# Four modulation chunks moved from layer 0's mixer to the end of its experts, the rest respread, and a scratch tile moved

## What is computed

```python
def adaln_layer(x, cond, g_mix, g_ffn, ada_w, ada_b, mixer, moe_params):
    mod = (silu(cond) @ ada_w + ada_b)[:, None, :]      # (1024) @ (1024 x 6144)
    sh1, sc1, g1, sh2, sc2, g2 = split(mod, 6)
    out, state = mixer(rms_norm(x, g_mix) * (1 + sc1) + sh1)
    x = x + g1 * out
    x = x + g2 * hier_moe(rms_norm(x, g_ffn) * (1 + sc2) + sh2, *moe_params)
```

## Time and profile before

| | before |
|---|---|
| median of 3 runs (lowest, highest) | 1665.0 us (1661.41, 1667.53) |
| the profiled execution, its own time | 1667.2 us |
| its span, first to last instruction | 1665.4 us |
| mean granted TensorE clock, as a share of 2.4 GHz | 0.947 |
| PE busy, DVE busy, ACT busy, POOL busy | 91%, 27%, 18%, 9% |
| HBM traffic | 319 GB/s over the span |
| layer 0: projection and mLSTM / attention and output / experts | to about 250 / 250 to 377 / 377 to 857 us |
| between the layers | 857 to 878 us |

### The profile page before, as it was taken

How to read it: one execution, slowest core, us unless ns; L and a number is a source line. 1 busy time by engine, 2 the same in 40 slices (tenths; PEclk the granted TensorE clock), 3 DMA queues, 4 the chain that set the end, 5 groups by cost and what they waited for, 6 DMA issues and landing times.

```text
span 1665.4 us, 21436 instructions
## 1 busy us (share of the span) xinstructions
PE 1516.3 (91%) x8387; PEld 723.5 (43%) x8387; DVE 445.5 (27%) x1055; ACT 304.9 (18%) x649; POOL 145.8 (9%) x200
## 2 busy tenths in 40 slices
PE   5999887979999999999958998896999999999991
PEld 4455784444433333333314555544333333333330
DVE  0012586433111111111123025633311111111113
ACT  3100225211111111111121005511111111111112
POOL 1002111100000000000005000100000000000001
PEclk9999887978999999999988999997999999999995
DMA  9999962245999999999969522103999999999982
GB/s 349 331 335 179 384 223 104 81 177 220 428 427 428 428 428 428 428 427 427 428 252 309 184 101 77 53 28 144 408 428 428 427 428 427 429 428 428 427 345 117
DMA packets 82919, 521.56 MB, mean 313 GB/s; under 512 B 10130, under 2 KB 11610, under 8 KB 56240
## 3 DMA queue, kind: packets, MB, share of 16 engines
q1 hardware_dynamic: 69536, 485.58, 71.4%
q0 software_dynamic: 13328, 35.22, 6.9%
HBM read 511.01 MB, written 20.22 MB: 319 GB/s over the span
## 4 chain that ended last, share of the span: by engine, by line
PE 88%; DVE 7%; ACT 2%; DMA 1%; issue 1%; POOL 0%; POOLq 0%; DVEq 0%; ACTq 0%
PE psum L896 26%; PE psum L909 14%; PE psum L877 10%; PE psum L543 6%; PE psum L842 5%; PE psum L565 5%; PE psum L562 3%; PE psum L902 3%; PE psum L467 2%; PE psum L889 2%; PE psum L883 2%; PE psum L764 1%; PE psum L509 1%; PE psum L751 1%; PE psum L789 1%
## 5 line engine op out<-in xcount | busy, mean ns | idle before, releaser
L896 PE MATMUL psum<-ring,area_t 128*64 128x512 f32 x1024 | 449.9, 592 | 1.8 <-issue 0.9
L897 PE MATMUL psum<-ring,area_t 128*64 128x512 f32 x1024 | 450.0, 593 | 0.0
L896 PEld LDWEIGHTS psum<-ring,area_t 128*64 128x64 f32 x1024 | 140.1, 137 | 291.8 <-issue 291.8
L909 PE MATMUL psum<-ring,area_t 128*64 128x512 f32 x1024 | 235.6, 602 | 2.3 <-DVE area_t L1864 2.3
L1835 DVE COPY area_q<-psum 64x512 f32<-64x512 f32 x64 | 44.4, 694 | 567.2 <-PE psum L897 567.2
L877 PE MATMUL psum<-area_h,area_t 128*64 128x512 f32 x768 | 180.8, 607 | 3.0 <-DVE area_t L1849 3.0
L2048 POOL DMA_INDIRECT pair_rows<-area_q,idx x64 | 62.4, 975 | 932.3 <-ACT area_q L1267 932.3
L897 PEld LDWEIGHTS psum<-ring,area_t 128*64 128x64 f32 x1024 | 140.2, 137 | 0.0
L909 PEld LDWEIGHTS psum<-ring,area_t 128*64 128x64 f32 x1024 | 69.1, 137 | 123.2 <-issue 123.2
L1257 ACT ACTIVATE area_q<-psum 64x512 f32<-64x512 f32 x64 | 37.8, 590 | 403.3 <-PE psum L897 403.3
L877 PEld LDWEIGHTS psum<-area_h,area_t 128*64 128x64 f32 x768 | 56.6, 140 | 113.7 <-issue 110.5
(11 more groups left out here) (265 smaller groups left out, 1396.7 us busy)
## 6 DMA issues: line engine op xcount, KB each, us to landing
ring<-in_moe_w SPq DMA_DIRECT2D x192, 2048.0 KB, 14.8
ring<-in_ada_w SPq DMA_DIRECT2D x24, 2048.0 KB, 20.0
ring<-in_na_w_in SPq DMA_DIRECT2D x6, 2048.0 KB, 17.2
ring<-in_ab_w_in SPq DMA_DIRECT2D x5, 2048.0 KB, 18.7
area_m<-mod_ready POOLq DMA_DIRECT2D x6, 1024.0 KB, 9.3
area_q<-pair_rows POOLq DMA_DIRECT2D x6, 1024.0 KB, 7.3
ring<-in_ab_w_out SPq DMA_DIRECT2D x2, 2048.0 KB, 20.8
area_g<-mod_ready POOLq DMA_DIRECT2D x4, 1024.0 KB, 8.8
```

The lines of the kernel that those rows point to most:

```text
L896: pe.matmul(banks[2 + u][0:64, :], lhsT, w1[:, k, :], start=(k == 0), stop=(k == KT - 1))
L897: mm = pe.matmul(banks[2 + u][64:128, :], lhsT, w3[:, k, :], start=(k == 0), stop=(k == KT - 1))
L909: mm = pe.matmul(banks[6 + u][64 * j:64 * j + 64, :], hidT[u][:, k, :], w2[:, k, 512 * j:512 * j + 512], start=(k == 0), stop=(k == 3))
```

## The change

The table of steps changes, four points of PE's program get a new `ada_step` or lose one, and ACT's copies, DVE's `modulation(5)` and POOL's round trip for group 5 move with it:

```diff
-        ADA_STEPS = ((("in", 0), 2), ... (("in", 4), 2), (("in", 5), 2), ("turned", 2), ("summed", 1), ("scored", 1), (("stage", 0), 1), (("stage", 1), 1), (("stage", 2), 2))
+        ADA_STEPS = ((("in", 0), 2), ... (("in", 4), 0), (("in", 5), 2), ("turned", 2), ("summed", 1), ("scored", 1), ("updated", 1), ("last", 1), ("gap", 4))
-        mixed = area_m[:, 4608:5632].rearrange("p (b n) -> p b n", b=2)
+        mixed = area_q[:, 4608:5632].rearrange("p (b n) -> p b n", b=2)
# stream: layer 1's list begins with the four chunks
             if l:
+                stream += [("ada",) + q for q in ADA_AT["gap"]]
                 stream += [("in", 1, c) for c in NA_ORDER]
# PE, project_na
+                pe.wait_ge(M["y_copied"], EXPERTS)
+                ada_step("gap")
# PE, mlstm: stage 2 behind direction 0; stage 0 ahead of the sums; the three stage steps go
                         if s == 2 and d == 0:
                             sums(s, 0)
+                            ada_step("last")
...
                             update_products(s, d)
+                        if s == 0:
+                            ada_step("updated")
                         sums(s, 0)
                         sums(s, 1)
-                        ada_step(("stage", s))
...
-                ada_step(("stage", 2))
# ACT, mlstm and finish_layer
+                    if s == 0:
+                        ada_copies("updated")
...
                         duplicate_keys()
+                        ada_copies("last")
...
+                    if l == 0 and t == 0:
+                        ada_copies("gap")
                     act.wait_ge(S["x_moe"], NT * l + t + 1)
# DVE: out of attention, to the start of layer 1
-                    if l == 0 and i in (5, 10):
-                        modulation(4 if i == 5 else 5)
+                    if l == 0 and i == 5:
+                        modulation(4)
...
                 if l:
+                    modulation(5)
                     copy_na()
# POOL: group 5's round trip, from the mLSTM's end to the start of layer 1
-            for G in range(4, 6):
-                store_ada(*divmod(G, 3))
-                finish_mod(G)
+            store_ada(1, 1)
+            finish_mod(4)
...
+                    store_ada(1, 2)
+                    finish_mod(5)
                     pool.wait_ge(S["h_ready"], NT * 3)
+                    pool.wait_ge(S["cmod_stored"], 160)
```

More of the change, by code:

```diff
@@ L271, in build @@
         over_landed = [sem(f"over{l}_landed") for l in range(2)]
-        ADA_STEPS = ((("in", 0), 2), (("in", 1), 2), (("in", 2), 2), (("in", 3), 2), (("in", 4), 2), (("in", 5), 2), ("turned", 2), ("summed", 1), ("scored", 1), (("stage", 0), 1), (("stage", 1), 1), (("stage", 2), 2))
+        ADA_STEPS = ((("in", 0), 2), (("in", 1), 2), (("in", 2), 2), (("in", 3), 2), (("in", 4), 0), (("in", 5), 2), ("turned", 2), ("summed", 1), ("scored", 1), ("updated", 1), ("last", 1), ("gap", 4))
         ADA_AT, ADA_GROUPS = {}, {}
@@ L291, in build @@
                 stream.append(("in", 0, _step[1]))
-            stream += [("ada",) + q for q in ADA_AT[_step]]
+            if _step != "gap":
+                stream += [("ada",) + q for q in ADA_AT[_step]]
         for l in range(2):
             if l:
+                stream += [("ada",) + q for q in ADA_AT["gap"]]
                 stream += [("in", 1, c) for c in NA_ORDER]
@@ L440, in _ @@
             load_overflow(0)
-            for n in range(NUM["in", 1, NA_ORDER[0]], NUM["moe", 1, 0]):
+            for n in range(NUM[("ada",) + ADA_AT["gap"][0]], NUM["moe", 1, 0]):
                 if n == NUM["in", 1, NA_ORDER[1]]:
@@ L573, in turn_na @@
                 if n == 0:
+                    pe.wait_ge(S["ada_copied"], 5)
                     pe.wait_ge(S["na_ctx_loaded"], 16)
@@ L716, in turn_queries @@
                     pe.wait_ge(S["ctx_v"], 16)
-                    pe.wait_ge(S["ada_copied"], 5)
+                    pe.wait_ge(S["ada_copied"], 4)
                 for t in range(NT):
@@ L1170, in mlstm @@
                         b_squares(2)
-                    ada_copies(("stage", s))
+                    if s == 0:
+                        ada_copies("updated")
                     if s == 1:
@@ L2072, in _ @@
                 if l == 0:
-                    pool.wait_ge(S["cmod_stored"], 160)
+                    pool.wait_ge(S["cmod_stored"], 128)
                 load_G(l, 0)
```

## The result

The changed kernel takes 1668.96 us (median of 6 runs, 1668.52 to 1672.93), the kernel before on the same chip 1666.0: ratio 1.0028, 95% interval 1.0015 to 1.0042. So the change costs about 3 us where a gain of 0.3 us was forecast. That is a small slowdown inside the forecast range, but neither interval holds 1.0000, the ratio of no change. All ratios here compare fast runs with fast runs; one run of e3, 3183.21 us, was slow and is not in its ratio.

What follows compares the result with a forecast made beforehand. The chain was taken as 88% PE, so moving chunks off it should pay: -6.2 us in layer 0 and +5.9 between the layers give -0.3 us, forecast 1664.7 us, range 1657.0 to 1672.0.

Steps and rivals of the forecast that it cites:

- Projection, -3.7: Projection's end: PE loses two ada chunks and all of their 3.7 us counts.
- mLSTM stages, -1.7: mLSTM stages 0 and 1: two single chunks move into PE's gaps, shortening DVE's waits by 1.7 us together.
- mLSTM's end, -0.6: Between mLSTM and attention: two chunks go, but attention waits for the state stores, so only 0.6 us is gained.
- rival B: mLSTM's end: state stores do not hold attention back, so about 7 us counts instead of 0.6; 1658.3 us, chance 0.17.
- PE idle for some 5 us: Sign expected ahead of ACT's first copy of attention, with that copy at 251 to 252 us.
- Start of attention: Layer 0: ACT's first copy of attention was to come at 251 to 252 us instead of 257.12.
- Attention, -0.2: Attention: DVE loses three tiny operations of modulation(5), about 0.2 us less.
- Layer 0 together, -6.2: Layer 0 up to its experts: projection, mLSTM, mLSTM's end and attention sum to 6.2 us less.
- Between the layers, PE nothing: Between the layers: four chunks, at most 14.6 us, fit PE's idle 21.24 us and cost PE nothing.
- Transfers, +5.9: Between the layers: queued weight chunks slow the last scatter by 3.2 us and each pair megabyte by 1.9; 5.9 us more.
- Rival D: Between the layers: the queue costs more than layer 0's 6.2 us, up to 13.4, 1672.2 us; chance 0.17.
- Rival C: Between the layers: pair traffic is let through, the queue costs only 0 to 3 us, about 1660 us; chance 0.13.

Runs made afterwards that it cites:

- e3: Kernel before plus four unused 2 MB loads between the layers, ahead of layer 1's projection chunks; 1675.7 us, ratio 1.0045 to the kernel before.
- e5: Kernel before with the mLSTM's n and m stores issued later, during layer 1's attention; 1664.6 us, ratio 0.9986 to the kernel before.
- e10: Kernel before plus two unused 2 MB loads between the layers; 1668.4 us, ratio 1.0008 to the kernel before.
- e12: Kernel before run again unchanged, for a second profile; 1665.6 us, ratio 0.9998.
- e1: Changed kernel run again unchanged, for a second profile; 1668.6 us, ratio 1.0019 to the kernel before.
- e2: Changed kernel with its four chunk loads between the layers cut to an eighth, products and waits kept; 1664.5 us, ratio 0.9984 to the kernel before.
- e4: Changed kernel with the mLSTM's n and m stores issued later, during layer 1's attention; 1664.2 us, ratio 0.9986 to the kernel before.
- e6: Changed kernel with the four chunks at the mLSTM's end instead of between the layers; 1668.3 us, ratio 1.0012 to the kernel before.
- e9: Changed kernel with the four chunks in layer 0's output projection and routing, n and m stored later; 1653.7 us, ratio 0.9929 to the kernel before.
- e11: Kernel before plus four unused 2 MB loads issued only when the last scatter has landed; 1671.5 us, ratio 1.0024 to the kernel before.
- e8: Changed kernel with the four chunks in layer 0's output projection and routing instead of between the layers; 1659.1 us, ratio 0.9947 to the kernel before.
- e7: Changed kernel with the four chunks at the mLSTM's end and n and m stored later; 1661.8 us, ratio 0.9975 to the kernel before.

## Why the prediction was wrong

*Projection, -3.7.* Right. From the first projection product to the mLSTM's first piece all six profiles with the old steps take 112.5 us, the eight others 108.7: -3.8.

*mLSTM stages, -1.7.* Wrong. From the mLSTM's first piece to POOL's issue of the C store, just ahead of n's, it is 66.9 to 68.1 us in the six profiles with the old mLSTM (first, e3, e5, e10 to e12; mean 67.4) and 67.1 to 69.7 in the eight with the new one (first, e1, e2, e4, e6 to e9; mean 68.3): 0.9 longer, though the two ranges overlap. The chunk ran in the gap at the high clock, as hoped (1.95 us at 205.77), but then PE had nothing until DVE was done. Windows 40 us behind the mLSTM's first piece, at about the same work, in the first profiles before and changed:

```profile
213.60:218.60 5.00, 3.39 (x31) 3.20 (x30) 4.61 (x8) 0.00 (x0) 0.00 (x0) 1.00 1.06 396
```

```profile
214.40:219.40 5.00, 4.21 (x20) 3.91 (x20) 4.21 (x10) 0.00 (x0) 0.00 (x0) 0.50 0.78 334
```

The granted clock there is 0.50 instead of 1.00, and the products on which DVE waits take up to twice as long (2.07 us at 213.31, 1.21 before). My bound of 0, "a chunk at the low clock in a gap gives the wait back", named another piece: the chunk was not slow, the work behind it was. But that this costs the time is not shown. e11 has the old mLSTM, 0.50 in this window too and one of the shortest stretches (67.0 us to the C store); e4 has the new mLSTM, 0.98 there and 67.1. Why the 1.7 us did not come stays open.

*mLSTM's end, -0.6.* The mechanism is right, and with it rival B falls: attention waits for the stores, whose landing is there to the tenth of a microsecond (e4). The size is lost in the scatter: the n store is issued 13.3 us before attention's first copy in the changed kernel (first, e1, e2: 11.9 to 14.3) and 13.4 with the two chunks (first, e3, e10 to e12: 12.4 to 14.5). Rival B's 8.5 us were never PE time alone (e5). Two readings were wrong. "The engines are busy with something" is not what the profile shows: from 247.5 to 254.5 us it has a single packet in the kernel before, one of the instruction queue. And the sign "PE idle for some 5 us" does not follow from my own terms: products that end at 246.80 - 5.4 = 241.4 and a copy at 251 to 252 leave 9 to 10 us. 9.4 to 11.7 were found.

*Start of attention.* Forecast 6.0 us earlier, found 2.3: 192.0 us behind the first projection product (three profiles, 189.7 to 193.6) instead of 194.3 (five, 192.9 to 196.1). In these same profiles the mLSTM takes 1.6 us longer up to the n store, and -3.8 + 1.6 - 0.1 is this -2.3.

*Attention, -0.2.* Here 3.4 us came that I had not seen: 123.6 us from its first copy to the first expert product instead of 127.0. DVE's work on attention is 0.7 us shorter; the rest is spread over attention and the output projection and is not settled. The cut at attention's first copy is a soft one: e1, which starts attention 3 to 4 us earlier than the other two profiles of the changed kernel, takes 125.5 us from there, they 122.2 and 123.0. e6, whose chunks stand ahead of attention again, takes 127.1.

*Layer 0 together, -6.2.* 315.6 us (315.2 to 315.8) instead of 321.3 (318.0 to 324.1) from the first projection product to the first expert product, so -5.7. The sum held by luck, since two misses cancelled: the mLSTM gave nothing, and attention gave 3.4 us that I had not seen.

*Between the layers, PE nothing.* Right: PE idles 16 us behind its last chunk.

*Transfers, +5.9.* This is the step that failed. The sum of a to d grew from 21.3 to 29.0: **+7.7**. The scatter's landing was taken from a neighbour, 3.2; it cost 4.4. The pairs were priced by bandwidth, 4.8 us a megabyte from the start of the kernel, 1.9 more for each. The first paid 3.3 and the second only 0.3. So my sum followed the second megabyte (7.0 less 1.1 of slack), where in fact the first decides: 4.4 + 3.3 = 7.7. What costs is the beginning of each transfer behind which something waits, not its share of the engines once it runs. The Trainium skill's rule on packets (DMA: Bandwidth & Descriptors, Queues, rings and completion order) fits the share that the pairs then had. They got 86.2% of the engines' time beside the weights' 17.2%, and the second megabyte came in 3.2 us. But the 4.3 us that the prediction drew from it for the whole stretch were still further off, since they price the share as well. The same page of the Trainium skill (Latency and other measured facts) names a longer memory access at high load, up to 2 us. The trace agrees in direction at most and shows 3 to 4.5 us for each transfer.

-5.7 + 7.7 = +2.0 us, against 3.2 us measured in twelve runs, interval 1.3 to 5.0. It is inside the interval; the 1.2 us between are not explained. Rival D's point of decision, 6.2 us, was passed, though its mechanism, a scatter behind the whole queue at 13.4 us, did not happen. Rival C is out. The chances had 0.17 for a queue that costs more than layer 0 gives; since my sum stood 0.3 us from that point (5.9 against 6.2) with terms taken from neighbours, that was too little.

## What to carry to other kernels

Price a small transfer that something waits for by its start, not by its bytes: beside a full weight queue each link of a chain store, wait, load cost 3 to 4.5 us more here, so prefetches belong where no such chain runs. Ask which of several transfers the chain follows before you add them up. Fill an engine's gap where it waits for another engine: the gap behind a DMA stall was a stall for the filling too (e6), while the filled gap ahead of the ranks' products even gave time back (2.5 to 4.2 us in e8, with a higher clock behind it). And compare marks within a profile: here one and the same kernel differed by 4 us in its start.

## What the runs showed of the hardware

- Behind a store of 1024 elements of 4 bytes (new_mlstm_n, 4 KB) and one of a few more (new_mlstm_m) there were 6 to 10 us in which next to nothing moved, and hardly a DMA engine was busy in the profile (0 to 16 GB/s from 251 to 259 us in the changed kernel, 0 from 245 to 251 in e1, at most 16 from 245 to 255 in the kernel before). POOL's wait for mod_raw was 9.0 to 11.6 us with them and 1.9 to 6.1 without (1.9 in e5, 4.2 in e7, 4.8 in e9, 6.1 in e4).
- PE's stream halted there too, with nothing in the profile that it waits for: up to 4.69 us in e6, 0.97 to 1.58 us at the longest in the five profiles with two chunks and the stores there, and not at all in e5 and e7, where the stores stand elsewhere. What PE lacks there was not tried. In the kernel before the only packet from 247.5 to 254.5 us is one of the instruction queue, at about 250 us, inside the first of the two holes.
- Four 2 MB loads issued together with a waited-for transfer delayed it as much as loads in flight (first scaling 9.08 us behind the issue in e11, 8.59 in the changed kernel, 5.22 and 5.45 alone).
- PE's granted clock over the ranks' products was 0.50 in e1, behind 6.69 us of idleness, and 1.00 in e8, behind two chunks and 1.85 us of idleness. In the mLSTM it was 0.50 behind 3.71 us of idleness in the changed kernel, and 1.00 or 0.50 in profiles with the same old mLSTM (first, e11).
- The same products of one kernel took 3.65 or 5.35 us in different profiles (the last expert's), and 10.54 or 12.0 to 12.2 us (projection chunk 0).
